# The place of one GpSimd add among the weight splits of the ranking stages of a two-block model

## What is computed

```python
q = (xt @ w_q).reshape(n, 8, 2, 128)                     # 8 heads, two halves
s = einsum('nhpd,hpkd->nhpk', q, keys)                   # 128 keys for each half
sv, si = top_k(s, 16)
cand = sv[:, :, 0, :, None] + sv[:, :, 1, None, :]
cs, ci = top_k(cand, 16)                                 # 16 experts a head
gate = softmax(cs)
a = einsum('nd,nhkd->nhk', xt, u[eidx])
out = einsum('nhk,nhkd->nd', gate * gelu(a), v[eidx])
```

## Time and profile before

| | |
|---|---|
| median of 3 runs | 3811.76 us (3808.01 to 3813.99) |
| profiled execution | 3813.3 us |
| its span, first to last instruction | 3811.5 us |
| granted TensorE clock, mean | 0.98 |
| PE busy | 3620.6 us, 95% |
| DVE busy | 2698.6 us, 71% |
| ACT busy | 1711.8 us, 45% |
| POOL busy | 698.4 us, 18% |

### The profile page before, as it was taken

The page is one execution under the profiler, slowest core; times in us unless marked ns, Lnnn a source line. Parts: engine busy times, 40 slices in busy tenths (PEclk is TensorE's granted clock), DMA queues, the critical chain, the costliest instruction groups (busy, mean ns, idle before and its releaser), DMA issues. The chain is left out here.

```text
span 3811.5 us, 57545 instructions
## 1 busy us (share of the span) xinstructions
PE 3620.6 (95%) x21555; PEld 3183.0 (84%) x21555; DVE 2698.6 (71%) x5248; ACT 1711.8 (45%) x2741; POOL 698.4 (18%) x668
## 2 busy tenths in 40 slices
PE   8997999989999986999999999999978999999998
PEld 8875888877878866988999999999966998888887
DVE  5674656656554769897888758888566887777776
ACT  4454445445543544553232333232245554555554
POOL 0001000000010104574444313333010650000000
PEclk9998999999999998999999999999989999999999
DMA  7556656565542123357888858888422366555664
GB/s 268 184 210 236 227 187 219 186 237 197 187 146 95 55 80 122 122 210 293 304 314 297 322 185 321 303 309 308 177 95 69 126 267 230 210 213 218 215 217 165
DMA packets 166767, 793.59 MB, mean 208 GB/s; under 512 B 16897, under 2 KB 58465, under 8 KB 97281
## 3 DMA queue, kind: packets, MB, share of 16 engines
q1 hardware_dynamic: 120496, 603.89, 43.3%
q0 software_dynamic: 45744, 186.36, 13.7%
q10 hardware_dynamic: 288, 0.15, 0.0%
HBM read 740.41 MB, written 47.28 MB: 207 GB/s over the span
## 5 line engine op out<-in xcount | busy, mean ns | idle before, releaser
L247 DVE TENSOR_TENSOR units<-ring,units 128x1024 fp32r<-128x1024 f32 x869 | 1063.5, 1226 | 522.8 <-ACT units L240 522.0
L240 ACT ACTIVATE units<-ring 128x1024 fp32r<-128x1024 f32 x928 | 978.1, 1056 | 897.9 <-PE ps L277 746.0
L276 PE MATMUL ps<-units,weighted 128*128 128x512 f32 x1280 | 501.4, 392 | 0.0
L275 PE MATMUL ps<-units,weighted 128*128 128x512 f32 x1280 | 499.4, 390 | 1.1 <-DVE units L247 1.1
L277 PE MATMUL ps<-units,weighted 128*128 128x512 f32 x1280 | 500.3, 391 | 0.0
L275 PE MATMUL ps<-wide_four,units 128*128 128x384 f32 (+1 forms) x1240 | 405.4, 327 | 6.0 <-PEq L3755 4.9
L277 PE MATMUL ps<-wide_four,units 128*128 128x384 f32 (+1 forms) x1240 | 403.6, 325 | 0.0
L276 PE MATMUL ps<-wide_four,units 128*128 128x384 f32 (+1 forms) x1240 | 403.0, 325 | 0.0
L277 PEld LDWEIGHTS ps<-units,weighted 128*128 128x128 f32 x1280 | 240.3, 188 | 51.1
L275 PEld LDWEIGHTS ps<-units,weighted 128*128 128x128 f32 x1280 | 240.9, 188 | 46.1 <-DVE units L247 1.5
L276 PEld LDWEIGHTS ps<-units,weighted 128*128 128x128 f32 x1280 | 240.7, 188 | 43.6
(11 more groups left out here) (592 smaller groups left out, 7640.8 us busy)
## 6 DMA issues: line engine op xcount, KB each, us to landing
ring<-in_stream SPq DMA_DIRECT2D x469, 1024.0 KB, 4.9
quad_ring<-in_mod_w POOLq DMA_DIRECT2D x12, 4096.0 KB, 14.7
gates_dram<-gates_place SPq DMA_DIRECT2D x20, 2048.0 KB, 7.2
gates_place<-gates_dram SPq DMA_DIRECT2D x15, 1536.0 KB, 13.2
gates_place<-gates_dram SPq DMA_DIRECT2D x15, 1024.0 KB, 5.9
gain_rows<-in_norm_gains SPq DMA_DIRECT2D x6, 512.0 KB, 5.1
peer_keys<-in_keys SPq DMA_DIRECT2D x3, 1024.0 KB, 6.4
gates_place<-gates_place SPq DMA_DIRECT2D x20, 128.0 KB, 2.0
```

Source lines behind the costliest of these rows:

```text
L240: act.activation(K.parts(n)[0], K.raw(n), ACT.Copy).then_inc(K.sig("hi_made").sem, units_to(K, n))
L247: dve.tensor_tensor(lo, K.raw(n), hi.bitcast(FP32), ALU.subtract).then_inc(K.sig("unit_split").sem, units_to(K, n))
L275: pe.matmul(out, w[0], x[0], start=start, stop=False)
L276: pe.matmul(out, w[0], x[1], start=False, stop=False)
```

## The change

It moves the add of L3429 from behind the split of unit `first_u + 1` to behind the last split of the loop (unit 20 in the first stage with experts, unit 22 in the second). Nothing else differs; the first ranking call has no such add.

```diff
                 pool.wait_ge(K.sig("unit_split").sem, n0 + 4)
                 for n in range(4, units):
                     split_lo(K, pool, n0 + n)
-                    if n == first_u + 1 and whole is not None:
+                    if n == units - 1 and whole is not None:
                         out, hi, lo = whole
                         pool.tensor_tensor(out, hi, lo, ALU.add).then_inc(K.sig("columns_joined").sem, 1)
                 pool.wait_ge(K.sig("unit_split").sem, n0 + units)
                 if whole is not None:
                     pool.wait_ge(*K.sig("columns_joined").at(1))
```

## The result

The changed kernel takes 3822.67 us (median of 11 runs, 3818.72 to 3824.52) against 3811.79 us (11 runs, 3808.01 to 3814.20): ratio 1.0029, 95% interval 1.0020 to 1.0037. That is +10.9 us, slower by 0.29%; forecast were +10.0 us and 3821.8. The profiled execution took 3823.0 us with a span of 3821.2, 9.7 above the span of before.

The account below looks back on a forecast made before the run. PE bounds most of the kernel, but DVE's tail bounds the second stage's end and, beyond 2.5 us late, the first's. Terms 6.7 + 2.95 + 0.35 gave +10.0 us on 3811.76: 3821.8 us, range 3817.5 to 3825.5.

Parts of the forecast that it names:

- PE's wait for POOL at L275: Second stage: PE lost 0.26 us once to the old add's place; that gap closes, worth 0 directly.
- a hold to 0.28 us behind the add's end: DVE's tail: L3618, with two SBUF inputs, is blocked for the add's whole length; tail 6.60 and 2.95 us late.
- The rival of a short hold at 2.1 us: DVE's tail: a long add lets DVE in after 2.1 us; +2.1 us, 3813.9; chance 0.07.
- the add meets nothing: DVE's tail: L3618 or later instructions slip through, adds lie in POOL's idle time; 3811.5 us; chance 0.10.
- The first stage's term: First stage with experts: tail 6.60 us late, PE stops 4.27 us, last group ends 6.7 us later (bounds 5.5 and 7.6).
- The cover of 2.48 us: First stage with experts: DVE has the gates ready 2.48 us before PE, so only a later tail bounds the stage.
- the lower bound that I worked out from the fourth product: First stage: +5.5 us if the clock stays up; DVE's last product ends at 1626.81 and one group of 1.06 follows.
- The clock is the difference: PE's gates-to-last-group stretch: 6.49 us without a stop, 8.88 and 9.81 behind stops, because the granted clock is lower there.
- The second stage's term: Second stage with experts: L3618 ends 2.95 us late and PE already waits, so +2.95 us (bounds 2.95 and 3.9).
- The upper variant without the 0.26: Second stage: +3.25 us if the last split does not come 0.26 us sooner.
- the 0.35 us that I added for it: Next block: PE starts slower behind a longer stop, mostly hidden by DVE's comparisons; +0.35 us (bounds 0 and 1).
- DVE goes first in the first stage: First stage: L3618 beats the add, POOL is held to the tail's end, block 4.1 us later; total +7.1, 3818.9; chance 0.08.

Follow-up runs that it names:

- The wait-for-the-tail run: Against the changed kernel, both adds late, POOL first waits for DVE's last product (L3654) before its late add; 3818.85 us, one run.
- the kept-awake run: Changed kernel plus unread PE transposes while it waits for the gates (36 first, 49 second stage with experts); 3818.18 us, ratio 1.0023 against 3812.27.

## Why the prediction was right

**Where the adds land.** Forecast 0.16 us ahead of L3618 in the first stage and 1.59 in the second; they were 0.19 and 1.76 ahead. The splits of the second stage were somewhat earlier than reckoned, which took 0.17 us off the hold there. PE's wait for POOL at L275 is gone, and as forecast it was worth nothing.

**What an add does to DVE.** Forecast was a hold to 0.28 us behind the add's end. It was 0.28 in the first stage (1614.16 against 1613.88) and 0.28 in the second (3031.66 against 3031.38). The gates came 1619.46 - 1607.12 = 12.34 us behind the tail's start, 6.62 later than before (forecast 6.60), and 2.79 later in the second stage (2.95). The rival of a short hold at 2.1 us is out, and so is "the add meets nothing": L3618 was held although it reads one tile twice.

**The first stage's term** was +6.7 and measured +7.35 by the yardstick. Two things in it were off. The cover of 2.48 us, measured at the gates, was not the one that counts: the third product had 0.45. With the clock up, the stage would have lost 6.60 - 0.45 = 6.15, and not 5.5, the lower bound that I worked out from the fourth product; the kept-awake run lost 6.27. And the stretch behind a stop of 4.14 us was 9.55 us, nearer to the 9.81 behind the stop of 23.93 than to the 8.88 behind 2.40 that I took as nearest. The stop's length doesn't order these stretches: behind 5.70 us, in the second stage, it was 9.08.

**"The clock is the difference"** was wrong as a cause. I gave all of the 2.39 us between 6.49 and 8.88 to the clock. At a granted clock of 1.00 the stretch is still 8.43 us, because PE waits for DVE's first and third product. The clock had 0.45 of the 2.39; the rest is that PE comes for the products as soon as the gates are ready, where in the first stage of before it came late enough to find them done. The number was right all the same, because the stretch that I took it from has the same waits in it.

**The second stage's term** was +2.95 and measured +3.00: 2.79 of hold and 0.20 of clock (9.08 for 8.88). A hold that was 0.16 shorter and a clock term that I had left to the bounds made up for each other. (The upper variant without the 0.26 is 2.95 + 0.26 = 3.21, and not the 3.25 of the prediction.)

**The next block.** For the 0.35 us that I added for it the traces give no measure. In the profiled pair the block behind the first stage took 1.42 us longer and the one behind the second 0.10 (85.09 in place of 84.99), but behind stages that nothing had been changed in these blocks took 122.49 and 123.73, and 83.34 to 84.99. That 9.65 + 0.35 came so near to the 10.35 of the two stages is partly luck: a first stage taken 0.7 too small and a term that nothing here shows.

**The rivals.** That DVE goes first in the first stage did not happen, and the runs say that little hung on it: where DVE had its turns between pieces, the delay was 6.71 and not 4.1. The wait-for-the-tail run gives what that rival had described, an add that is held to the tail's end: +3.9 us in the first stage. The prediction had 4.1; by its own terms (1627.1 + 0.5 - 1623.77) it is 3.8.

## What to carry to other kernels

An idle engine is not a free place for work that shares a path with another engine: ask what the neighbour does in those microseconds. The add was free beside one-input ranking instructions, and it held a tail of two-input and fast one-input ones for all that was left of it, at the one point of the stage where VectorE was what everything waited for. Measure a cover at the last consumer that waits, not at the first: here 2.48 us at the gates were 0.45 at the third product. And when TensorE is made to wait, count the slower clock behind the wait (1.3 us of 10 here), and don't give the clock what is a wait for the next operand.

## What the runs showed that I had not expected

- A VectorE instruction that GpSimd holds need not get in when the holding instruction ends. It waited out an add and the split queued behind it (5.30 us), the pieces left of eight (4.12) and pieces with a split behind them (6.30). In one case it got a turn behind each of eight pieces; there it always came within 0.25 us of a piece's start. Cutting the work into pieces is therefore no cure: 22.80 and 19.23 us in place of 23.44 and 18.76.
- A one-input shift on uint32 (L3623) is held too, and already by a memset, which reads nothing.
